# Branch b of a hybrid layer: gated y kept by partition in memory, and the work between the products reordered

## The reference

```
h  = RMSNorm(x) * (1 + scale1(c)) + shift1(c)
u  = h @ w_in      -> pool_in | z | xBC | dt | gate_a | gate_b
A  = pooling mixer: for windows 2, 4, 8, 16 (one for each 256 channels) mean - identity,
     then a 256x256 map per group and a scale;  a_out @ w_branch_a
B  = Mamba-2 mixer: causal conv, chunked scan (chunks of 64 in the reference), D skip,
     y * silu(z), grouped RMSNorm, times ssm_norm_w;  b_out @ w_branch_b
x += gate1(c) * ((sigmoid(gate_a) * A + sigmoid(gate_b) * B) @ w_out)
x += gate2(c) * SwiGLU(RMSNorm(x) ...);   final RMSNorm
```

## Time and profile before

| what | value |
|---|---|
| median of three runs | 2367.92 us (2366.45 to 2371.62) |
| the profiled execution | 2365.28 us |
| its span | 2363.6 us |
| PE, DVE, ACT, POOL busy | 96%, 53%, 26%, 5% |
| mean granted TensorE clock | 0.985 |

### The profile page before, as it was taken

How to read it: one execution, slowest core, us unless ns; L and a number is a source line. 1 busy time by engine, 2 the same in 40 slices (tenths; PEclk the granted TensorE clock), 3 DMA queues, 4 the chain that set the end, 5 groups by cost and what they waited for, 6 DMA issues and landing times.

```text
span 2363.6 us, 35843 instructions
## 1 busy us (share of the span) xinstructions
PE 2274.4 (96%) x13607; PEld 2178.4 (92%) x13607; DVE 1262.3 (53%) x2028; ACT 610.6 (26%) x1028; POOL 112.6 (5%) x177
## 2 busy tenths in 40 slices
PE   7999999999999999998998999999999999999995
PEld 3899999999999999988998997899999999999994
DVE  3565555556777777775666455524443334443345
ACT  6312122223333333331113333311111111111111
POOL 1000000000111111101000000100000000000000
PEclk9999999999999999999999999999999999999996
DMA  7456423335455556536342433211111111111104
GB/s 243 119 166 185 139 79 91 90 91 167 147 172 169 171 168 209 172 105 195 114 137 75 142 118 134 72 45 45 44 44 44 44 44 38 46 41 44 44 27 160
DMA packets 319361, 258.83 MB, mean 110 GB/s; under 512 B 13379, under 2 KB 293125, under 8 KB 319295
## 3 DMA queue, kind: packets, MB, share of 16 engines
q1 hardware_dynamic: 261968, 203.58, 28.5%
q10 hardware_dynamic: 53343, 41.84, 5.8%
q0 software_dynamic: 3984, 12.52, 1.5%
HBM read 195.69 MB, written 62.21 MB: 109 GB/s over the span
## 4 chain that ended last, share of the span: by engine, by line
PE 51%; issue 44%; DVE 2%; DMA 1%; ACT 1%; POOL 1%; SPq 0%; POOLq 0%; ACTq 0%; DVEq 0%
PE PS L1059 28%; PE PS L1276 12%; PE PS L1238 3%; PE PS L1228 1%; PE PS L1231 1%; DMA ada_first<-in_w_ada 1%; PE PS L1213 1%; PE PS L1256 1%; DVE pool_s L1900 1%; PE PS L1097 1%; PE PS L1161 1%; PE PS L1114 1%; PE PS L1169 1%; ACT xt L712 0%; DVE y_lo L1786 0%
## 5 line engine op out<-in xcount | busy, mean ns | idle before, releaser
L1487 DVE TENSOR_TENSOR w_lo<-w_raw,w_hi 128x1024 fp32r<-128x1024 f32 x156 | 190.7, 1222 | 380.7 <-ACT w_hi L670 379.8
L1415 PE MATMUL PS<-act_c_hi,w_hi 128*128 128x364 f32 (+1 forms) x1056 | 346.9, 329 | 1.2 <-ACT silu_g L1008 1.2
L1415 PE MATMUL PS<-act_c_lo,w_hi 128*128 128x364 f32 (+1 forms) x1056 | 346.9, 329 | 0.0
L1415 PE MATMUL PS<-act_c_hi,w_lo 128*128 128x364 f32 (+1 forms) x1056 | 346.9, 328 | 0.0
L1059 PE MATMUL PS<-act_a_hi,w_hi 128*128 128x364 f32 (+1 forms) x936 | 308.7, 330 | 1.4 <-ACT raw L787 1.3
L1059 PE MATMUL PS<-act_a_lo,w_hi 128*128 128x364 f32 (+1 forms) x936 | 307.5, 329 | 0.0
L1059 PE MATMUL PS<-act_a_hi,w_lo 128*128 128x364 f32 (+1 forms) x936 | 307.5, 328 | 0.0
L670 ACT ACTIVATE w_hi<-w_raw 128x1024 fp32r<-128x1024 f32 x156 | 164.6, 1055 | 444.8 <-PE PS L1059 194.2
L2080 DVE SCALAR_TENSOR_TENSOR f_acc<-PS,mods,f_acc 128x364 f32<-128x364 f32 (+1 forms) x352 | 164.3, 497 | 73.3 <-PE PS L1437 73.3
L1415 PEld LDWEIGHTS PS<-act_c_hi,w_hi 128*128 128x128 f32 x1056 | 198.5, 188 | 1.6 <-ACT silu_g L1008 0.9
L1415 PEld LDWEIGHTS PS<-act_c_lo,w_hi 128*128 128x128 f32 x1056 | 198.5, 188 | 0.0
(11 more groups left out here) (264 smaller groups left out, 3891.3 us busy)
## 6 DMA issues: line engine op xcount, KB each, us to landing
w_raw<-in_w_in SPq DMA_DIRECT2D x64, 512.0 KB, 5.3
acs_in<-acs_c SPq DMA_DIRECT2D x36, 512.0 KB, 5.2
ada<-in_w_ada SPq DMA_DIRECT2D x16, 1024.0 KB, 7.6
gp_s<-gp ACTq DMA_DIRECT2D x24, 544.0 KB, 3.4
w_raw<-in_w_ffn_gate SPq DMA_DIRECT2D x22, 512.0 KB, 3.8
w_raw<-in_w_ffn_up SPq DMA_DIRECT2D x22, 512.0 KB, 3.9
w_raw<-in_w_ffn_down SPq DMA_DIRECT2D x22, 512.0 KB, 3.4
xs_in<-xs_c SPq DMA_DIRECT2D x36, 256.0 KB, 2.9
```

The costliest lines, as they stand in the source:

```text
L1415: e = pe.matmul(PS[:, n, 0:w], w_split[v][a][:, k * P:(k + 1) * P], act_c[b][:, k, o:o + w], start=(k == 0 and q == 0), stop=(k == KT - 1 ...
L1487: dve.tensor_tensor(w_split[v][1][:, :], w_raw[v][:, :], w_split[v][0][:, :].bitcast(F32), ALU.subtract)\
```

## The change

- `y_c` is laid out by f and partition: row (f, p) holds all 36 chunks. Stores write rows of 512 B; `y_again` is four DMAs, one for each f, with rows of 1088 columns (4352 B), and no fifth. `y_high` waits for its half of them only.
- ScalarE hands the banks over to branch b after its own last copy out of them, in place of VectorE.
- `y_high` and `y_low` of the next group are made earlier: for group 1 ScalarE makes all four at q = 1, VectorE one after each of pieces 4 to 7; for groups 2 and 3 ScalarE makes two each at q = 1 and 2, VectorE one after each of pieces 3 to 6.
- `window_sums` is cut into `window_start` and `window_add`, placed one by one after the thirds of pieces 0 and 1, 4 and 5 (in group 0: pieces 4 and 5, 6 and 7); `means` follows the second third of the second piece.
- The pooled splits of groups 0 and 1 are made inside the last group of branch b (pieces 2, 3, 6 and 7), and VectorE then waits for its last copy before it frees the pooling product's banks.
- The two FFN units are split after the sixth of the looped norm2 steps, not before the first.

```
-    y_c = dram("y_c", (GROUPS * NCH, 4, P, CH))
+    y_c = dram("y_c", (4, P, GROUPS * NCH * CH))
...
+                    sp.dma_start(y_in[g % 2][:, f, :], y_c[f, :, g * NCH * CH:g * NCH * CH + T])\
+                      .then_inc(y_back[g % 2][f // 2], 16)
...
             def y_high(g, f):
-                act.wait_ge(y_back[v][0], 48 * (g // 2) + 48)
-                if f > 1:
-                    act.wait_ge(y_back[v][1], 32 * (g // 2) + 32)
+                act.wait_ge(y_back[v][f // 2], 32 * (g // 2) + 32)
...
+                    if last and k == 1:
+                        act.wait_ge(mm_free["ssd"], 75)
+                        act.sem_inc(mm_free["brb"], 3)
...
                     if g == 0:
-                        if q == 2:
+                        if q == 1:
                             for f in range(4):
                                 y_high(1, f)
                     elif g < GROUPS - 1:
-                        if not q:
+                        if q == 1:
                             act.wait_ge(mm["brb"], 24 * g)
-                        y_high(g + 1, q)
-                    elif q == 2:
-                        pooled_parts(0)
+                        if q in (1, 2):
+                            y_high(g + 1, 2 * q - 2)
+                            y_high(g + 1, 2 * q - 1)
+                    elif q in (1, 2):
+                        pooled_parts(q - 1)
...
-            hi(U_FFN, 0, "bra", 3 * KT)
-            hi(U_FFN + 1, 1, "bra", 3 * KT)
...
             with act.Fori(0, 3) as i:
                 norm2_step(i * 2 + 1, 1)
                 norm2_step(i * 2 + 2, 0)
+            hi(U_FFN, 0, "bra", 3 * KT)
+            hi(U_FFN + 1, 1, "bra", 3 * KT)
...
             def branch_b_start():
 
-                dve.wait_ge(mm_free["ssd"], 75)
                 dve.wait_ge(gp_store[1], 12 * 16)
-                dve.sem_inc(mm_free["brb"], 3)
...
+            def window_add(j, k):
+
+                if k <= j // 2:
+                    cur, nxt, first = [pool_s1, pool_s0][k % 2] if k else pool_x, [pool_s0, pool_s1][k % 2], (2 << k) - 1
                     pstep(dve.tensor_tensor(nxt[:, first:full], cur[:, first:full], cur[:, first - (1 << k):full - (1 << k)],
                                             ALU.add))
...
+                        j = 2 * g + (piece >= (4 if g else 6))
+                        for n in range(3):
+                            branch_b_third(g, q, m, n)
+                            if piece in ((0, 4) if g else (4, 6)):
+                                if n == 0:
+                                    window_start(j)
+                                else:
+                                    window_add(j, n)
+                            elif piece in ((1, 5) if g else (5, 7)):
+                                if n == 0:
+                                    window_add(j, 3)
+                                elif n == 1:
+                                    means(j)
+                        if g == 0:
+                            y_low(1, piece - 4)
+                        elif g < GROUPS - 1 and 3 <= piece < 7:
+                            y_low(g + 1, piece - 3)
+                        elif g == GROUPS - 1 and piece in (2, 3, 6, 7):
+                            pooled_part(piece // 4, piece % 2)
+
+            dve.wait_ge(mm_free["brb"], 24 * GROUPS + 3)
             dve.sem_inc(mm_free["pool"], 3)
...
-                if gi < GROUPS - 1:
+                if 0 < gi < GROUPS - 1:
                     pooled_parts(gi + 1)
...
-            lo(U_FFN, 0)
-            lo(U_FFN + 1, 1)
...
             with dve.Fori(0, 3) as i:
                 norm2_step(i * 2 + 1, 1)
                 norm2_step(i * 2 + 2, 0)
+            lo(U_FFN, 0)
+            lo(U_FFN + 1, 1)
```

More of the change, by code:

```diff
@@ L364, in y_out @@
             def y_out(t, k):
-                sp.dma_start(y_c[t].rearrange("f p l -> p f l"), yg[k][:, :, :]).then_inc(y_store[k], 16)
+                sp.dma_start(y_c[:, :, ds(t * CH, CH)].rearrange("f p l -> p f l"), yg[k][:, :, :]).then_inc(y_store[k], 16)
             def y_again(g):
                 for f in range(4):
[L370 to L374, removed]
+                    sp.dma_start(y_in[g % 2][:, f, :], y_c[f, :, g * NCH * CH:g * NCH * CH + T])\
+                      .then_inc(y_back[g % 2][f // 2], 16)
             def y_normed_out(t, k):
@@ L606, in _ @@
             pool.wait_ge(yn_ready, GROUPS * NCH + 1)
-            pool.dma_start(y_c[GROUPS * NCH - 1].rearrange("f p l -> p f l"), yg[2][:, :, :]).then_inc(y_last, 16)
+            pool.dma_start(y_c[:, :, (GROUPS * NCH - 1) * CH:].rearrange("f p l -> p f l"), yg[2][:, :, :]).then_inc(y_last, 16)
             at_s = SEQ + 2 * PW
@@ L936, in _ @@
                     hi(U_POOL + 1, 1, "brb", 96)
-                else:
+                elif gi > 1:
                     pooled_parts(gi)
@@ L1844, in branch_b_start, with branch_b_third @@
             def branch_b_start():
-                dve.wait_ge(mm_free["ssd"], 75)
                 dve.wait_ge(gp_store[1], 12 * 16)
-                dve.sem_inc(mm_free["brb"], 3)
-            def branch_b_sums(g, q, m):
[L1852 to L1860, removed]
+            def branch_b_third(g, q, m, n):
+                s0 = 24 * g + 6 * q + 3 * m
+                o, w = SUBS[n]
+                dve.wait_ge(mm["brb"], s0 + n + 1)
+                dst = acc[:, 2 * q + m, o:o + w]
+                if g == 0:
+                    dve.tensor_copy(dst, PS[:, n, 0:w]).then_inc(mm_free["brb"], 1)
+                else:
+                    dve.wait_ge(mm_free["brb"], s0 + n - 20)
+                    dve.tensor_tensor(dst, PS[:, n, 0:w], dst, ALU.add).then_inc(mm_free["brb"], 1)
+            def branch_b_sums(g, q, m):
+                for n in range(3):
+                    branch_b_third(g, q, m, n)
             dve.wait_ge(dt_act, 8)
@@ L1887, in pstep, with window_start @@
                 dve.wait_ge(pl_vec, count[0])
-            def window_sums(j):
+            def window_start(j):
                 dve.wait_ge(pool_x_in, 32 * (j + 1))
@@ L1895, in window_sums @@
                 pstep(dve.tensor_copy(pool_tail[:, 1, :, j], pool_x[:, full - PW:full]))
-                cur, first = pool_x, 0
-                for k in range(j // 2 + 1):
-                    nxt, first = [pool_s0, pool_s1][k % 2], first + (1 << k)
+                window_add(j, 0)
+            def window_add(j, k):
+                if k <= j // 2:
+                    cur, nxt, first = [pool_s1, pool_s0][k % 2] if k else pool_x, [pool_s0, pool_s1][k % 2], (2 << k) - 1
                     pstep(dve.tensor_tensor(nxt[:, first:full], cur[:, first:full], cur[:, first - (1 << k):full - (1 << k)],
                                             ALU.add))
-                    cur = nxt
             def means(j):
@@ L1946, in _ @@
                     for m in range(2):
-                        branch_b_sums(g, q, m)
                         piece = 2 * q + m
[L1949 to L1963, removed]
+                        j = 2 * g + (piece >= (4 if g else 6))
+                        for n in range(3):
+                            branch_b_third(g, q, m, n)
+                            if piece in ((0, 4) if g else (4, 6)):
+                                if n == 0:
+                                    window_start(j)
+                                else:
+                                    window_add(j, n)
[4 more added lines that the diff above has]
+                                    means(j)
+                        if g == 0:
+                            y_low(1, piece - 4)
[4 more added lines that the diff above has]
+            dve.wait_ge(mm_free["brb"], 24 * GROUPS + 3)
             dve.sem_inc(mm_free["pool"], 3)
```

## The result

The changed kernel takes 2350.35 us (median of 4 runs, 2347.01 to 2352.0) against 2368.57 for the kernel before beside it: ratio 0.992, 95% interval 0.9903 to 0.9938, so 18.2 us faster. I had forecast 24.8 less. The profiled execution took 2347.01 us, span 2345.0 (before 2363.6), the fastest of the four.

What follows compares the result with a forecast made beforehand. TensorE, busy 96% of the span, bounds the kernel, so only its idle and slow-clock time counts. Terms -2.8 -5.4 -0.8 -3.8 -4.5 -1.5 +1.6 -1.2 -0.8 -5.6 = -24.8 give a median of 2343.1 us, range 2338 to 2351.

Steps and rivals of the forecast that it cites:

- rival 1: y_in does not land sooner, so TensorE loses 4.2 us in piece 5 of the first group; time 2347.3, chance 0.15.
- Rival 2: New short waits and the clock eat 6.4 us of the gain; time 2349.5, chance 0.16.
- Entry: Start of branch b: ScalarE hands over the banks earlier; idle -2.1 us, clock -0.7, sum -2.8.
- First group, splits one ahead: End of branch b's first group: TensorE idles 2.2 us instead of 7.58, -5.4; half a clock fall saved, -0.8.
- Later groups: Between branch b's later groups: y_low ends a piece early, so two waits of 1.88 us go, -3.8.
- Pooling sums: Sums placed between thirds in branch b: three waits go, -4.5 us, and the clock loss behind the 2.27 one, -1.5.
- Pooling product: Start of the pooling product: 1.87 us idle falls to 0.7, -1.2, and the 0.78 wait goes, -0.8.
- The new waits for pool_x: Sums in branch b wait for loads of tiles 1 and 2: +0.8 us each (tile 2 up to +2.1), sum +1.6.
- y by partition: y_in loads with 4352 B rows: landing taken 5 us sooner (0 to 6.8), no gain alone, cover for earlier splits.
- Output projection: Later FFN splits: 4.61 us wait before the third projected tile goes, -4.5; clock -1.7, late xr +0.6; sum -5.6.
- Rival 3: VectorE parks on pool_x inside a piece; slower than before from a landing of 15.8 us on; chance 0.04.
- Rival 4: No effect: the idle time returns in the next stage because the FFN is bound elsewhere; chance 0.03.

Runs made afterwards that it cites:

- b3: Changed kernel with SP issuing the y_in loads of group 2 only once pool_x of tile 2 has landed; 2346.68 us, ratio 0.9905.
- a1: Changed kernel with the old layout of y_c and the old five loads, all else as changed; 2349.47 us, ratio 0.992.
- a2: Changed kernel with two pool_x buffers, so tile j+1 is loaded while tile j is summed; 2341.56 us, ratio 0.9886.
- a4: Changed kernel with the last y_low of group 1 moved from behind piece 7 to behind its first third; 2350.91 us, ratio 0.9925.
- b2: Changed kernel with two pool_x buffers, the earlier last y_low of group 1, and tile 2's sums one piece later; 2341.28 us, ratio 0.9887.
- c2: Changed kernel with ScalarE's hi(U_B+3) ahead of the four y_high of group 1, nothing else; 2344.55 us, ratio 0.9907.
- a3: Kernel before with only the two FFN units' splits moved behind the sixth looped norm2 step; 2361.48 us, ratio 0.9969.
- c1: b2 with ScalarE's hi(U_B+3) ahead of the four y_high of group 1; 2338.91 us, ratio 0.988.
- b4: Kernel before with only the layout of y_c changed (stores, loads and waits of y_high); 2368.25 us, ratio 1.0002.
- b1: Changed kernel with both a2 (two pool_x buffers) and a4 (last y_low of group 1 earlier); 2345.07 us, ratio 0.9904.

## Why the prediction was right or wrong

The sign and most of the mechanisms held, and 2350.35 lies in the range, 0.65 us from its end. It lies outside the 2338.5 to 2346 of the likeliest case; only the places given to rivals 1 and 2 reach that far. Between the profiled executions the working is 18.3 us of the 18.6 measured: idle time -18.4, clock -2.2, and +2.2 in the stretch ahead of branch b, where the diff changes only the rows of y's stores and where nearly all of it, 2.0, is clock. Those 2.2 are luck, against the forecast; the parts themselves fell 4.2 us short.

- **Entry**: -2.06 us idle and -0.76 clock (2.43 of lost work became 1.67), forecast -2.1 and -0.7. Right.
- **First group, splits one ahead**: TensorE's idle time 2.24, forecast 2.2. The clock fell all the same, so the -0.8 that I took as half a fall was -0.03. I had ordered the falls by the length of the idle stretch; the kernel before shows that length does not order them: its 2.50 us at the start of the output projection brought a fall, its 2.79 us in the pooling product none.
- **Later groups**: both waits gone, -3.76. **Pooling sums**: the three gone, -4.45 and the fall behind them -1.49. **Pooling product**: -1.10 and -0.78. All right.
- **The new waits for pool_x**: the step that failed. Tile 1 cost 0.93 (forecast 0.8), tile 2 2.66 and a fall of 1.70 (forecast 0.8, bound 2.1, no fall): 5.3 us instead of 1.6. The mechanism, a load waited for inside a piece, was right, its size was not. I took the landing from the eight loads seen before and the middle of their range. But tile 2's load was itself the slowest of the eight (7.5 us), at this very place beside the y_in loads, so by my own formula 2.1 and not 0.8 was its price with nothing new. Then the new layout issued those loads in 1.76 us where they had taken 4.9, and it became 9.7. My working of the layout counted what faster issue does for y_in and not what it does to its neighbour. b3 shows the cause; with the old rows (a1) the load took 7.4 us and the wait was 0.15. At 9.7 my formula gives 4.3 us; it was 2.66, as the bank was wanted 1.7 us later than I had it (11.9 us after the last piece's end, not 10.2), after the fall that I had counted by half.
- **y by partition**: for the landing I took 5 us sooner. The 2.8 in the 6.8 behind it was misread: I set the last y_in load (9.4) against the median of four pooled_in loads (6.6), whose own last one took 8.7. It is the issue that became shorter (four in 2.03 us; three of the old took 5.95); from its own issue the last load took 8.8 us against 9.4, and 8.8 to 13.0 over the eight profiled kernels with the new layout and new order. In the profiled execution the cover held by half a us (copy done at 1087.6, bank wanted at 1088.1); in a2, a4, b2 and b3 TensorE lost 0.8 to 3.6 us there (0.8, 2.1, 3.6 and 2.9). The Trainium skill (DMA: Bandwidth & Descriptors, Specifications) has 512 B as the least transfer at line rate, by which the rows are equal once issued; 8.8 against 9.4 agrees with it better than my 5 us did. So **rival 1** was right in part: y_in lands no sooner from its own issue, and its wait is there in some executions, at 0.8 to 3.6 us and not 4.2. That it is there in the other three runs of the changed kernel (2349.43 to 2352.0, against 2347.01 for the one profiled) was not seen, only argued from c2, whose four runs lie within 2.3 us and whose median is 5.8 us lower.
- **Output projection**: -4.46 idle and -1.63 clock, with none of the +0.6 for xr. Forecast -5.6, measured -6.1, alone (a3) -6.5.
- **Clock as a whole**: -2.2, forecast -4.7. 0.8 of it is the half fall, 1.7 the one behind pool_x. A fall after the 2.79 us of the pooling product (1.71) is new, one after 2.50 us at the start of the output projection (1.70) is gone; neither wait changed.
- **Rival 2** (new short waits and the clock take 6.4 us, time 2349.5) came nearest in number, and two of its parts came: no clock gain at the first group's end, and pool_x later than I had it. The other two did not (the clock gain at entry came, xr cost nothing), and 2.2 us of the shortfall are the stretch ahead of branch b, so that its number is this near is in part luck. **Rival 3**, VectorE parked on pool_x, was this same wait at a landing of 9.7 and not 15.8. **Rival 4** fell: from TensorE's first wait in the FFN to the end it is 834.2 us, against 834.5 before.
- **The signs**: all of TensorE's came, with 2.66 where a short wait was named. y_in landing under 7 us did not come (8.8). A wait of over 3 us on pool_x was to mean "wrong": TensorE's was 2.66, but VectorE stood 5.45 us on it. The last y_high ended over 2 us past the start of piece 4, which was the other such sign; but my own working had it 2.5 us past (E-21.5 against E-24), so that sign was set too tight.

## What to carry to other kernels

When loads are made cheaper to issue, list what else is in flight at the time of issue and price that as late, not only the loads as early: here it made a neighbour's landing 9.7 us out of 7.1 or 7.4. When a landing is priced from several seen before, look for the one at the same place first, and compare a last load with a last load. A second buffer (a2) took 8.8 us off with the same work, of which its trace explains 4.6. When an engine makes the inputs of the next stage ahead of time, put what is wanted first ahead of what only might have landed: the fastest kernel here (c1) does, and its trace has no wait there. A cover that holds by half a us in one profile is no cover; look at the same landing in several executions.

## What the runs showed of the hardware

- A store and a load of 512 KB on POOL's queue took 3.0 and 4.1 us alone, and 7.7 and 9.7 us with four 544 KB loads (rows of 4352 B, issued in 1.76 us) and two 512 KB ones issued on SP's queue around them. With the four in rows of 512 B, issued over 4.9 to 6 us, they took 6.4 and 7.1 (the kernel before) and 5.5 and 7.4 (a1).
- One y_in load, the last of four, landed 8.8 to 13.0 us after its issue in eight kernels whose code up to it is all but the same.
- Whether the clock falls after the same idle time differs between executions. After the 2.50 us at the start of the output projection it fell in the kernel before, a1, a3, b3, b4 and c1, not in the changed kernel, a2, a4, b1, b2 and c2; after the 2.79 us of the pooling product it fell in the changed kernel, a1, a2, a4, b1, b2 and c1, not in the kernel before, a3, b3, b4 and c2; after the 1.25 us at entry always, after the 2.24 us before the second group always (the changed kernel, a1, a2, b3 and c2), after the 1.88 us between groups never. Up to 1050 us, where the kernels differ at most in the rows of y's stores, the loss ranged from 1.4 us (the kernel before) to 7.0 (a1). So one profile of each kernel doesn't tell what a small change does to the clock.
